# An encoder layer with a mixture of experts: the last token tile's router ahead of its shared expert, shorter block tables, and the expert stage's first fetches issued inside the stage before it

## The reference, cut to what matters

```python
def moe(u, p):                                # u: 2048 tokens x 1024
    scores = jax.nn.sigmoid(xt @ p['w_router'])            # 64 experts
    ...                                       # bias, best 4 of 8 groups
    _, idx = lax.top_k(jnp.where(expert_mask, choice, -jnp.inf), TOP_K)   # 6
    w = jnp.take_along_axis(scores, idx, axis=1)
    w = w / jnp.sum(w, axis=-1, keepdims=True) * ROUTED_SCALE
    routed = routed_experts(xt, idx, w, p['w_exp_in'], p['w_exp_out'])
    shared = swiglu(xt, p['w_sh_in'], p['w_sh_out'])
    return routed + shared

def routed_experts(xt, idx, w, w_exp_in, w_exp_out):
    ...                     # entries (token, weight) sorted by expert, each
    padded = (counts + MOE_BLOCK - 1) // MOE_BLOCK * MOE_BLOCK   # 128
    def body(acc, blk):     # expert's list padded to blocks of 128 entries
        tok, gw, e = blk
        yb = swiglu(xt[tok], w_exp_in[e], w_exp_out[e]) * gw[:, None]
        return acc.at[tok].add(yb), None
```

## Time and profile before

| | before |
|---|---|
| median of 3 runs | 2974.78 us (2974.44 to 2975.02) |
| profiled execution: its time / its span | 2974.65 us / 2972.8 us |
| mixing stage's tables written (SP issues `s_block`) | 1480.83 us into the span |
| expert stage's first instruction | 1489.2 us |
| PE starts `first(0)` / `first(1)` | 1518.63 us / 1529.33 us |
| expert blocks (adds of `ex_y` into `s_acc`) | 130 |

### The profile page before, as it was taken

The page is one execution under the profiler, slowest core; times in us unless marked ns, Lnnn a source line. Parts: engine busy times, 40 slices in busy tenths (PEclk is TensorE's granted clock), DMA queues, the critical chain, the costliest instruction groups (busy, mean ns, idle before and its releaser), DMA issues. The chain is left out here.

```text
span 2972.8 us, 31554 instructions
## 1 busy us (share of the span) xinstructions
PE 2756.4 (93%) x9158; PEld 1323.8 (45%) x9158; DVE 1590.4 (53%) x2573; ACT 697.4 (23%) x1222; POOL 1103.6 (37%) x1151
## 2 busy tenths in 40 slices
PE   7999999899999899899559999999999999999990
...
DMA packets 189230, 466.53 MB, mean 157 GB/s; under 512 B 21850, under 2 KB 46746, under 8 KB 187738
## 3 DMA queue, kind: packets, MB, share of 16 engines
...
...
## 5 line engine op out<-in xcount | busy, mean ns | idle before, releaser
L1683 PE MATMUL ex_pH<-ex_wi,ex_xT 128*128 x2096 | 945.1, 594 | 13.7 <-DVE ex_xT L1596 12.4
L1538 POOL DMA_INDIRECT ex_xg<-s_u,ex_gidx x536 | 599.6, 1119 | 165.5 <-issue 160.2
L1683 PEld LDWEIGHTS ex_pH<-ex_wi,ex_xT 128*128 128x128 f32 x2096 | 388.7, 191 | 454.9 <-issue 454.9
L1700 PE MATMUL ex_pY<-ex_wo,ex_hT 128*128 x1040 | 467.5, 592 | 0.0
L1596 DVE STREAM_TRANSPOSE ex_xT<-ex_xg 128x1024 f32<-128x1024 f32 x132 | 164.2, 1244 | 358.2 <-DMA ex_xg<-s_u,ex_gidx 358.1
L1700 PEld LDWEIGHTS ex_pY<-ex_wo,ex_hT 128*128 128x128 f32 x1040 | 197.6, 190 | 248.7 <-issue 248.7
L1557 POOL DMA_INDIRECT s_acc<-ex_y,ex_sidx x130 | 211.9, 1630 | 187.1 <-DVE ex_y L1634 121.7
L1634 DVE SCALAR_TENSOR_TENSOR ex_y<-ex_pY,ex_wgt,ex_G 128x1024 f32<-128x1024 f32 x130 | 166.9, 1284 | 184.9 <-PE ex_pY L1700 164.7
L1585 ACT ACTIVATE ex_hT<-ex_pG 128x256 f32<-128x256 f32 x130 | 49.9, 384 | 869.5 <-PE ex_pG L1670 862.8
L638 PE MATMUL fr_pF<-fr_uT,fr_wf 128*128 128x512 f32 x512 | 224.9, 595 | 1.3 <-ACT fr_uT L332 1.3
L1600 DVE TENSOR_TENSOR ex_h<-ex_silu,ex_pH 128x256 f32<-128x256 f32 x131 | 54.7, 418 | 309.1 <-ACT ex_silu L1576 303.9
...
## 6 DMA issues: line engine op xcount, KB each, us to landing
...
```

The lines of the kernel that those rows point to most:

```text
L1538: nc.gpsimd.indirect_dma_start(xg[:, u, g, :], None, u2_q, bass.IndirectOffsetOnAxis(ap=gidx[:, u, g:g + 1].bitcast(U32), axis=0)).then_in ...
L1683: m = nc.tensor.matmul(pH[:], xT[:, u, k, :], wi[:, bass.ds(slot, 1), k, :].rearrange("p a f -> p (a f)"), start=(k == 0), stop=(k == KD - 1))
L1700: m = nc.tensor.matmul(pY[:, h, :], hT[:, c, :], wo[:, bass.ds(slot, 1), c, h * 512:(h + 1) * 512].rearrange("p a d -> p (a d)"), start=(c ...
```

## The change

In words, by engine:

- **PE**: for the last tile the logits (into `pL`, which is free by then) come right after the transposes of `ut`, and the ranks of tiles 15 and 16 around the shared expert's first product. The count for `tables` (`M` plus `Msum`, into `pL`) no longer waits for the last slots. The shared expert's rest follows after it.
- **ACT**: for the last tile the `Exp` comes ahead of the shared expert's SiLU; `ez` has two buffers.
- **DVE**: at the end `gate` and `add_shared` of the last tile no longer stand ahead of its ranks and router. `slots` and `entry` have two buffers. `tables` is rewritten: the block count by rounding in 3 operations instead of 17, and both halves of the block table in one pass. `places` is new: the difference of the gate rows (before in the expert stage) and the first block's row numbers.
- **SP**: the weights of expert 0 (3 MB) are loaded after the last `s_u` store. The two gate rows come at tile 9. After the tables, four transfers read the first block's 128 token numbers from the list, once for each quarter of the partitions (`ids`).
- **POOL**: after the last scatter it fetches `raw` by the block table in SBUF, and gathers block 0's rows. Its first gather in the expert stage is that of block 1.
- **Memory**: the weights' ring, `wo` and `lruT` share one tensor, and other tensors of the mixing stage are handed on (`left`), so that these transfers have a place to land.

```diff
+                    for b in range(NB):
+                        sp.dma_start(gates[:, b, :], gate2(b)).then_inc(gate_in, 16)
...
+            sp.wait_ge(pl_mm, NT)
+            sp.wait_ge(pa_mm, NT)
+            sp.dma_start(first_w[:, 0, :, :], exp_weights[0][0].rearrange("(k p) f -> p k f", p=P)).then_inc(w_in_exp[0], 16)
+            sp.dma_start(second_w[:, 0, :, :], exp_weights[1][0].rearrange("(c p) d -> p c d", p=P)).then_inc(w_in_exp[0], 16)
+            sp.wait_ge(z_ready, NT)
+            sp.dma_start(acc_d[(NT - 1) * P:, :][0:P, :], xt[:, (NT - 1) % NX, :]).then_inc(z_stored[(NT - 1) % NX], 16)
+            sp.wait_ge(tables_ready, 3)
+            sp.dma_start(count_d, cumi[0:1, :]).then_inc(tables_out, 16)
+            sp.dma_start(block_d.rearrange("a (c p) -> p (a c)", p=P), blk[:], allow_slow_non_contiguous=True).then_inc(tables_out, 16)
+            for r in range(2):
+                sp.wait_ge(listed[r], 16 * TOP_K * NT // 2)
+            for q in range(4):
+                sp.dma_start(ids[32 * q:32 * q + 32, :].unsqueeze(2), list_d[0:P, 0:1].rearrange("(g j) c -> j g c", g=4), allow_slow_non_contiguous=True).then_inc(ids_in, 16)
...
+            pool.wait_ge(tables_ready, 1)
+            passed(pool, apart)
+            for c in range(2):
+                nc.gpsimd.indirect_dma_start(raw[:, c, :, :].rearrange("p t c -> p (t c)"), None, list_d.rearrange("(b t) c -> b (t c)", t=P),
+                                             bass.IndirectOffsetOnAxis(ap=blk[:, c:c + 1].bitcast(U32), axis=0)).then_inc(raw_in, 16)
+            for r in range(2):
+                pool.wait_ge(u2_stored[r], 16 * NT // 2)
+            pool.wait_ge(gidx_ready, 1)
+            passed(pool, apart)
+            for g in range(4):
+                nc.gpsimd.indirect_dma_start(xg[:, 0, g, :], None, u2_d.rearrange("t (a f) -> (t a) f", a=4),
+                                             bass.IndirectOffsetOnAxis(ap=gidx[:, 0, g:g + 1].bitcast(U32), axis=0)).then_inc(gathered[0], 16)
...
+            for i in range(1, NT):
+                turned(i)
+                shared_expert(i)
+                scores(i, pB[:, LOG:LOG + N_EXP])
+            turned(NT)
+            scores(NT, pL[:, 0, 0:N_EXP])
+            shared_expert(NT)
...
             def tables():
-                dve.wait_ge(slots_ready, NT)
                 dve.wait_ge(count_mm, 1)
-                cnt, nblk, cum = M, ez, sg
-                step(nc.vector.tensor_copy(cnt[:], pB[:, RNK:RNK + N_EXP]))
-                step(nc.vector.tensor_scalar(nblk[:], cnt[:], 0.0, 1.0, ALU.mult, ALU.add))
-                for j in range(1, T // P):
-                    step(nc.vector.scalar_tensor_tensor(nblk[:], cnt[:], float(j * P), nblk[:], ALU.is_gt, ALU.add))
-                step(nc.vector.tensor_scalar(rk[:], nblk[:], 0.0, 1.0, ALU.mult, ALU.add))
-                step(nc.vector.tensor_tensor_scan(cum[:], rk[:], nblk[:], 0.0, ALU.mult, ALU.add))
-                step(nc.vector.tensor_copy(cumi[:, RING + 1:RING + 1 + N_EXP], cum[:]))
-                for c in range(2):
-                    step(nc.vector.tensor_scalar(sm[:, 2 + c:3 + c], tok0[:], float(c * P), None, ALU.add))
...
-                    nc.vector.tensor_copy(blk[:, c:c + 1], wk[:, 4 + c:5 + c]).then_inc(tables_ready, 1)
-                    nc.vector.tensor_copy(blk[:, 2 + c:3 + c], wk[:, c:c + 1]).then_inc(tables_ready, 1)
+                nblk, cum, pair = ez[:, 0, :], sg, lambda k: sm[:, k:k + 2]
+                by_block = lambda x: x.unsqueeze(1).to_broadcast([P, 2, N_EXP])
+                by_expert = lambda x: x.unsqueeze(2).to_broadcast([P, 2, N_EXP])
+                step(nc.vector.tensor_scalar(nblk, pL[:, 1, 0:N_EXP], 1.0 / P, 0.5 - 0.5 / P, ALU.mult, ALU.add))
+                step(nc.vector.tensor_scalar(nblk, nblk, float(2 ** 23), None, ALU.add))
+                step(nc.vector.tensor_scalar(nblk, nblk, -float(2 ** 23), 1.0, ALU.add, ALU.max))
+                step(nc.vector.tensor_scalar(rk[:], nblk, 0.0, 1.0, ALU.mult, ALU.add))
+                step(nc.vector.tensor_tensor_scan(cum[:], rk[:], nblk, 0.0, ALU.mult, ALU.add))
+                step(nc.vector.tensor_scalar(sm[:, 4:5], tok0[:], 0.0, None, ALU.add))
+                step(nc.vector.tensor_scalar(sm[:, 5:6], tok0[:], float(P), None, ALU.add))
+                over, part = junk[:, 0, 0:2, :], junk[:, 0, 2:4, :]
+                step(nc.vector.tensor_tensor(over, by_block(cum[:]), by_expert(pair(4)), ALU.is_le))
+                step(nc.vector.tensor_reduce(wk[:, 0:2], over, AX.X, ALU.add))
+                step(nc.vector.tensor_tensor(part, over, by_block(nblk), ALU.mult))
+                step(nc.vector.tensor_reduce(wk[:, 2:4], part, AX.X, ALU.add))
+                step(nc.vector.tensor_tensor(wk[:, 4:6], pair(4), wk[:, 2:4], ALU.subtract))
+                step(nc.vector.scalar_tensor_tensor(wk[:, 4:6], wk[:, 0:2], float(NT), wk[:, 4:6], ALU.mult, ALU.add))
+                step(nc.vector.tensor_scalar(wk[:, 4:6], wk[:, 4:6], float(N_EXP * NT), None, ALU.min))
+                nc.vector.tensor_copy(blk[:, 0:2], wk[:, 4:6]).then_inc(tables_ready, 1)
+                step(nc.vector.tensor_scalar(wk[:, 0:2], wk[:, 0:2], float(N_EXP - 1), None, ALU.min))
+                nc.vector.tensor_copy(blk[:, 2:4], wk[:, 0:2]).then_inc(tables_ready, 1)
+                nc.vector.tensor_copy(cumi[:, RING + 1:RING + 1 + N_EXP], cum[:]).then_inc(tables_ready, 1)
+            def places():
+                dve.wait_ge(gate_in, 32)
+                nc.vector.tensor_tensor(gates[:, 1, :], gates[:, 1, :], gates[:, 0, :], ALU.subtract).then_inc(gate_diff, 1)
+                dve.wait_ge(ids_in, 64)
+                nc.vector.tensor_scalar(gidx[:, 0, :], ids[:], 4.0, quad[:], ALU.mult, ALU.add).then_inc(gidx_ready, 1)
+                dve.wait_ge(gate_diff, 1)
...
+            ranks(NT - 2)
+            router(NT - 1)
+            gate(NT - 1)
+            ranks(NT - 1)
             tables()
+            add_shared(NT - 1)
+            places()
...
+            turn(NT)
+            pe.wait_ge(ut_copied, NT)
+            pe.wait_ge(l_added, NT)
+            logits(pL[:, 0, 0:N_EXP])
+            rank(NT - 1, NT - 1)
+            shared_in(NT)
+            rank(NT, NT)
+            nc.tensor.matmul(pL[:, 1, 0:N_EXP], ones, M[:], start=True, stop=False)
+            nc.tensor.matmul(pL[:, 1, 0:N_EXP], ones, Msum[:], start=False, stop=True).then_inc(count_mm, 1)
+            gated(NT)
+            shared_out(NT)
...
+            for r in range(RING):
+                if r:
+                    load(r, w_exp_in[r].rearrange("(k p) f -> p k f", p=P), w_exp_out[r].rearrange("(c p) d -> p c d", p=P))
+                    sp.wait_ge(w_in[r - 1], 32)
+                sp.sem_inc(w_ready, 1)
+            with sp.Fori(1, N_EXP // RING) as q:
...
             pool.wait_ge(quarter_ready, 1)
-            for b in range(2):
-                places(b, b)
-                gather(b, b)
+            pool.sem_inc(gidx_ready, 1)
+            places(1, 1)
+            gather(1, 1)
...
+        ring = sb("ring", [P, RING, KD, 2 * D_E])
+        part = lambda k, inner: ring[:, 2 * k:2 * k + 2, :, :].rearrange("p a k f -> p (a k f)").rearrange("p (w f) -> p w f", w=inner)
+        wo = part(0, 2).rearrange("p w (i d) -> p w i d", d=D)
+        lruT = part(1, KL)
...
+        first_w, second_w = ring, qT[:].rearrange("p r (c d) -> p r c d", d=D)
+        gates, xg = mrow[:, 0, :, :], kT[:].rearrange("p b g t -> p (b g t)").rearrange("p (u g f) -> p u g f", u=2, g=4)
+        raw = grow[:, 0:4 * P].bitcast(I32).rearrange("p (c t x) -> p c t x", c=2, x=2)
```

278 lines of the change are left out of this document (133 added, 145 removed).

## The result

The kernel after takes 2959.88 us (median of 5 runs, 2956.87 to 2960.83) against 2974.78 of before (5 runs): ratio 0.9947, interval [0.9936, 0.9958]. It is faster by 14.9 us, half of the 30.3 forecast. The profiled execution took 2960.4 us over a span of 2958.8.

The account below looks back on a forecast made before the run. The prediction saw PE as the bound except for 63 us nearly idle between mixing and expert stages. Gains of 10.5 and 21.8 us, less 2.0 between slots and stage end, gave 30.3: 2974.78 to 2944.5 us, range 2941 to 2952.

Parts of the forecast that it names:

- PE's unbroken stretches: Middle of the mixing stage and whole expert loop: PE is always busy, and the change adds or removes no matmul there.
- the last tile's order: End of the mixing stage: the last tile's slots are ready at 1459.2 in place of 1469.66, 10.5 us earlier.
- no wait of DVE for the SiLU: Last tile: the SiLU is done at 1456.2, needed by 1456.65, a margin of 0.5 us.
- the start of the expert stage: From the expert stage's start to `first(1)`: 18.2 us instead of 40.0, a gain of 21.8.
- the forecast's own signs of being wrong: DVE waiting for the SiLU, POOL for row numbers past 1477, `first(1)` for block 1's gather, or slower loop blocks.
- 2.0 for landing (the smallest landing of the earlier trace) 1469.3: End of mixing on POOL: the last scatters, issued by 1467.3, land 2.0 us later at 1469.3.
- its second rival: The four small reads wait behind `s_block`'s 512 writes: 2.7 us late, 2947.2; late cases together 0.24.
- The exit costs 0.5 (SP's wait ends at 1488.8, the next stage is at 1489.3): Mixing stage's exit: 0.5 us from the last gather's issue at 1480.3 to the expert stage at 1480.8.
- The third rival: Exit or next start costs more without the old cover: 2949.7 if awaiting gathers' landing, or 2947; late cases together 0.24.
- the new tables: DVE after the last slots: 20 dependent operations instead of 42, 4.8 us, done at 1464.0.
- the reads of the ids: SP's four transfers of 128 numbers after the scatters land: 5.3 us, between 3.7 and 8.0.
- The shorter tables alone are worth nothing: Mixing stage's end: the stage now ends later than `s_block`'s landing at 1474.0 for another reason, so shorter tables gain nothing.

Follow-up runs that it names:

- e1: Kernel after with SP's issues of `s_count` and `s_block` moved behind its four reads of the ids: 2953.48 us.
- e13: Kernel after with the block tables turned by TensorE and `s_block` written as 4 rows of 512 bytes, still ahead of the reads: 2951.44 us.
- e11: Kernel after with `s_count` and `s_block` issued behind the ids' reads and block 0's four gathers issued in the expert stage: 2956.77 us.
- e15: e14 without its last two drains inside the mixing loop: 2946.69 us.
- e14: Kernel after with `s_block` written as 4 rows and a GpSimd drain heading each mixing-loop round from the fourth on: 2945.97 us.
- e7: Kernel after with the block tables made by the 42 operations of before: 2961.86 us.

## Why the prediction was wrong

**Right:** that PE's unbroken stretches stay as they are; the last tile's order (slots at 1460.81, less 2.2 for the later start of the stage: 1458.6 against 1459.03); no wait of DVE for the SiLU (the first product took 8.88 us from 1447.07); `s_block`'s issue (1467.30, less 2.2: 1465.1, against 1466.4); the gathers' issue (5.8 against 5.7); the start of the expert stage, 18.35 from the stage's start to `first(1)` (1495.9 to 1514.25) against 18.2. One of the forecast's own signs of being wrong came true: POOL waited for the row numbers past 1477, until 1481.56.

**The step that failed first:** "2.0 for landing (the smallest landing of the earlier trace rows) 1469.3". The reads behind the scatters' completion went out at 1477.59, 7.8 us behind the last issue. The landing itself is short, 1.2 us in e1 and e13, even shorter than 2.0. What the forecast took to cost the scatters nothing was the neighbour: 512 writes of 4 bytes, issued by SP 1.5 us before the last scatter. Before the change they came 3 us after it. The forecast had this mechanism as its second rival, but only for the four reads on the same queue and with a price of 2.7 us. The scatters are on POOL's queue and were held all the same. The Trainium skill ("DMA: Bandwidth & Descriptors", Queues, rings and completion order) says that a semaphore's increment lands only after every earlier write of its DMA engine, across its queues. The traces agree: the increment came 10.0 to 11.0 us after the issue of the 512 pieces, and 1.2 us after the last scatter's with `s_block` behind the reads (e1) or in 4 pieces (e13). That fetches of POOL's queue landed up to 10 us late as well (e11 above) is more than that sentence says. Cost against the forecast: 7.8 − 2.0 = 5.8, and 0.7 for the scatters' own issue (one took 1.69 us instead of 0.96).

**The second:** "The exit costs 0.5 (SP's wait ends at 1488.8, the next stage is at 1489.3)". That was SP's exit, the last to arrive before. POOL's had ended 1.9 us earlier and was hidden by SP's wait for `s_block`; with `s_block` early and the last POOL work late, it ended the stage, 8.5 us behind the last issue (1487.37 to 1495.9). Cost 8.0. The third rival, an exit that costs more without the old cover, was the right place with a wrong mechanism (5.2 for the gathers' landing, which needs 1.8).

**Smaller:** the new tables have 18 operations and not 20, and took 4.1 us (1460.89 to 1464.97), not 4.8; the reads of the ids took 4.0 us (1477.59 to 1481.56) and not 5.3; the front's clock 2.2; and the loop lost 1.1, of which one pause of PE between 2700 and 2750 us (48.97 busy of 50) is 1.0.

In sum, `first(1)` is 15.25 late: 5.8 + 0.7 + 8.0 − 1.3 + 2.2 = 15.4, and −0.15 in the remaining steps (slots −0.4, gathers' issue +0.1, start of the stage +0.15). With both causes taken away e15's way is 39.83 against 40.0, and e14's 41.42. That e15 comes so near is partly luck: its exit still costs 3.0 us and not 0.5 (1479.33 to 1482.3), and what makes up for it is the scatters' landing (1.2 for 2.0), the reads (4.0 for 5.3) and a first product of 8.82 for 9.54. So two waits were missing from a chain whose other steps were right to within 1.3 us each.

"The shorter tables alone are worth nothing" was wrong too: e7 puts them at 3 to 4 us of the way. On TensorE's clock the runs differ. In after, behind the same transposes, the clock stayed at half through 1508 and the first product took 9.78 us; in e1 it stood at 0.92 and 0.93 from 1496 to 1500, as in the earlier trace rows, and the first product took 8.83. The Trainium skill ("TensorE: Matmul & The Clock Gate", Part 4: PE-mode transpose) says that transposes don't bring the full clock. After agrees with it and e1 does not; the other runs had 8.5 to 10.1 us, so it stays open.
